# One matmul fewer in each half of the forward transform's 16-bin tile, two sums by VectorE instead

## The reference

```python
def fftconv(v, kf, skip):
    L = v.shape[1]
    vf = jnp.fft.rfft(v.astype(jnp.float32), n=2 * L, axis=1)
    y = jnp.fft.irfft(vf * kf[None], n=2 * L, axis=1)[:, :L]
    return y + v.astype(jnp.float32) * skip.astype(jnp.float32)

def hyena_mixer(u, x1, x2, kf, skip):
    z = fftconv(u, kf[:, 0], skip[0])
    z = x1.astype(jnp.float32) * z
    z = fftconv(z, kf[:, 1], skip[1])
    z = x2.astype(jnp.float32) * z
    return z.astype(u.dtype)
...
m = g_a * (y_a @ w_a) + g_b * (y_b @ w_b) + g_c * (y_c @ w_c)
return h + m @ w_out
```

## Time and profile before

| What | Value |
|---|---|
| Runs | 1127.41, 1128.18, 1128.9 us (median 1128.18) |
| Profiled execution, its own time | 1127.34 us |
| Its span | 1125.5 us |
| Granted TensorE clock, mean | 0.999 |
| TensorE busy | 1103.2 us, 98% of the span |
| VectorE busy | 772.3 us, 69% |
| ScalarE busy | 567.1 us, 50% |
| GpSimd busy | 61.9 us, 5% |
| HBM traffic | 178 GB/s over the span |

### The profile page before, as it was taken

One profiled execution on the slowest core, in us unless ns is written; L12 is line 12 of the kernel. 1 busy time (PEld: TensorE's weight loads), 2 busy tenths in 40 slices (PEclk: granted clock), 3 DMA queues, 4 the chain that ended last, 5 costly groups with the idle time before them and its releaser, 6 DMA issues.

```text
span 1125.5 us, 17228 instructions
## 1 busy us (share of the span) xinstructions
PE 1103.2 (98%) x7158; PEld 1005.7 (89%) x7158; DVE 772.3 (69%) x1151; ACT 567.1 (50%) x787; POOL 61.9 (5%) x98
## 2 busy tenths in 40 slices
PE   4999999999999999999999999999999999999997
PEld 2999999999999999999999988888888888888885
DVE  6778888778787688886888785554555455454654
ACT  6655555556545456555554564443444444444443
POOL 4030000300001200002000000000000000000000
PEclk9999999999999999999999999999999999999999
DMA  8744443644335534435543475555555555556652
GB/s 315 241 135 169 150 151 122 205 169 150 135 128 197 186 116 147 151 125 185 188 150 117 160 269 195 202 188 198 187 187 187 192 197 189 201 194 255 231 189 110
DMA packets 30494, 201.54 MB, mean 179 GB/s; under 512 B 3873, under 2 KB 4193, under 8 KB 7745
## 3 DMA queue, kind: packets, MB, share of 16 engines
q1 hardware_dynamic: 25024, 180.16, 45.4%
q0 software_dynamic: 5248, 19.77, 5.3%
q10 hardware_dynamic: 144, 0.52, 0.1%
HBM read 195.19 MB, written 5.24 MB: 178 GB/s over the span
## 4 chain that ended last, share of the span: by engine, by line
PE 98%; DVE 1%; ACT 0%; DMA 0%; issue 0%; DVEq 0%; ACTq 0%
PE ps L574 30%; PE ps L575 30%; PE ps L576 30%; PE ps L579 2%; PE ps L598 1%; PE ps L687 1%; PE ps L727 1%; PE ps L617 1%; PE ps L618 0%; PE ps L718 0%; PE ps L719 0%; PE ps L930 0%; PE ps L729 0%; DMA net<-net_in 0%; PE ps L735 0%; PE ps L737 0%
## 5 line engine op out<-in xcount | busy, mean ns | idle before, releaser
L1328 DVE TENSOR_TENSOR w_lo<-raw,w_hi 128x1024 fp32r<-128x1024 f32 x336 | 409.0, 1230 | 257.8 <-ACT w_hi L988 257.3
L988 ACT ACTIVATE w_hi<-raw 128x1024 fp32r<-128x1024 f32 x336 | 351.2, 1056 | 342.3 <-PE ps L576 340.1
L574 PE MATMUL ps<-xn_hi,w_hi 128*128 128x272 f32 (+2 forms) x1280 | 367.5, 287 | 0.0
L575 PE MATMUL ps<-xn_lo,w_hi 128*128 128x272 f32 (+2 forms) x1280 | 365.7, 286 | 0.0
L576 PE MATMUL ps<-xn_hi,w_lo 128*128 128x272 f32 (+2 forms) x1280 | 365.5, 286 | 0.0
L574 PEld LDWEIGHTS ps<-xn_hi,w_hi 128*128 128x128 f32 x1280 | 242.2, 189 | 2.0
L575 PEld LDWEIGHTS ps<-xn_lo,w_hi 128*128 128x128 f32 x1280 | 241.8, 189 | 0.7
L576 PEld LDWEIGHTS ps<-xn_hi,w_lo 128*128 128x128 f32 x1280 | 242.1, 189 | 0.0
L574 PE MATMUL ps<-w_hi,xg_hi 128*128 128x512 f32 x352 | 137.4, 390 | 0.0
L576 PE MATMUL ps<-w_hi,xg_lo 128*128 128x512 f32 x352 | 137.2, 390 | 0.0
L575 PE MATMUL ps<-w_lo,xg_hi 128*128 128x512 f32 x352 | 137.1, 390 | 0.0
(11 more groups left out here) (265 smaller groups left out, 1394.6 us busy)
## 6 DMA issues: line engine op xcount, KB each, us to landing
raw<-w_stream SPq DMA_DIRECT2D x168, 1024.0 KB, 4.9
branch_y<-ystage POOLq DMA_DIRECT2D x12, 256.0 KB, 3.9
y_raw<-branch_y POOLq DMA_DIRECT2D x3, 1024.0 KB, 7.0
xin<-x SPq DMA_DIRECT2D x2, 1024.0 KB, 6.4
w4s<-w POOLq DMA_DIRECT2D x16, 128.0 KB, 6.0
absd<-decay POOLq DMA_DIRECT2D x8, 256.0 KB, 6.2
h<-x POOLq DMA_DIRECT2D x2, 1024.0 KB, 8.2
rows_t<-rpb POOLq DMA_DIRECT2D x8, 219.0 KB, 6.2
```

Source lines behind the costliest of these rows:

```text
L574: mm(out_ap, a_hi, b_hi, start=first, stop=False)
L575: mm(out_ap, a_hi, b_lo, start=False, stop=False)
L988: A(w_hi[:, w % 2, part, :], raw[:, w % 4, 1024 * part:1024 * part + 1024], ACT.Copy).then_inc(hi_done, 1)
L1328: return V.tensor_tensor(dst, src, hi.bitcast(F32), ALU.subtract)
```

## The change

The 16-bin tile of the forward transforms gets a function of its own. The table `sym` gets 160 more columns: the 16 high columns and the 16 low columns for each of the two outputs, arranged so that for each output `ri` 48 columns starting at `7 * L + 16 * ri` hold the high part, another block, and the low part. A matmul of these 48 columns with `uT_hi` writes high by high into PSUM rows 0 to 15 and low by high into rows 32 to 47; rows 16 to 31 are not used. A second matmul adds high by `uT_lo` into rows 0 to 15, a third adds the stacked rest, whose table columns are padded with zeros to 48. ScalarE copies rows 32 to 47 of both outputs to a new tile `extra` (16 x 512); VectorE adds rows 0 to 15 to it, and the two multiplications read `extra` in place of PSUM. A new semaphore `fx_half` goes from the copy to the sum.

```diff
@@ constants()
-    sym = two_parts(np.concatenate([even[:128], odd[:128], back[0], back[1]], axis=1),
-                    np.concatenate([np.concatenate([even[128:], none]), np.concatenate([none, odd[128:]]), back[2]], axis=1))
+    hi, lo = two_parts(np.concatenate([even[:128], odd[:128], back[0], back[1]], axis=1),
+                       np.concatenate([np.concatenate([even[128:], none]), np.concatenate([none, odd[128:]]), back[2]], axis=1))
+    extra_bins = [part[:, at:at + NM] for part in (hi, lo) for at in (0, L)]
+    extra_rest = [np.pad(hi[:, at:at + NM], ((0, 0), (0, 2 * NM))) for at in (4 * L, 5 * L)]
+    sym = np.concatenate([hi] + extra_bins + extra_rest, axis=1), lo
@@ build()
-    sym_hi = place("sym_hi", [128, 7 * L], F32R)
+    sym_hi = place("sym_hi", [128, 7 * L + 10 * NM], F32R)
...
+    extra = place("extra", [128, 2, CC])
...
-            load_table("sym", sym_in, sym_hi[:, :], sym_lo[:, :], 7 * L)
+            load_table("sym", sym_in, sym_hi[:, :], sym_lo[:, :], 7 * L + 10 * NM)
@@ TensorE
+            def forward_extra():
+
+                for ri in range(2):
+                    out_ap, wide_ap = (ps[0:n, 4, CC * ri:CC * ri + CC] for n in (NM, 3 * NM))
+                    col, rest = 7 * L + NM * ri, 7 * L + 4 * NM + 3 * NM * ri
+                    mm(wide_ap, sym_hi[:, col:col + 3 * NM], uT_hi[:, ri, :], start=True, stop=False)
+                    mm(out_ap, sym_hi[:, col:col + NM], uT_lo[:, ri, :], start=False, stop=False)
+                    last = stacked(wide_ap, sym_hi[0:STACK, rest:rest + 3 * NM], uT_hi[0:STACK, 2, :], False, True)
+                last.then_inc(fwd_mm, 1)
...
                     if t == 5:
                         pe.wait_ge(y_full, c * 6 + 1)
-                        forward(2, 4)
+                        forward_extra()
...
                     if t == 13:
                         pe.wait_ge(y_full, c * 6 + 4)
-                        forward(2, 4)
+                        forward_extra()
@@ ScalarE, spectra()
                     n = TOK[f][1]
+                    if f == 2:
+                        act.wait_ge(fwd_mm, c * 6 + (3 * order + 3))
+                        A(extra[0:NM, :, :].rearrange("p r n -> p (r n)"), ps[2 * NM:3 * NM, 4, :], ACT.Copy).then_inc(fx_half, 1)
                     act.wait_ge(y_full, c * 6 + (3 * order + f + 1))
@@ VectorE, spectra()
                     bank = ps[0:n, 4 + f % 2, :].rearrange("p (r n) -> p r n", r=2)
+                    if f == 2:
+                        dve.wait_ge(fx_half, c * 2 + order + 1)
+                        link(V.tensor_tensor(extra[0:NM, :, :], extra[0:NM, :, :], bank, ALU.add))
+                        bank = extra[0:NM, :, :]
```

More of the change, by code:

```diff
@@ L388, in build @@
         fwd_mm = sem("fwd_mm")
+        fx_half = sem("fx_half")
         y_full = sem("y_full")
```

## The result

| | Kernel before | Changed kernel |
|---|---|---|
| Median of 13 runs | 1128.5 us (1127.41 to 1129.07) | 1130.69 us (1130.08 to 1131.52) |
| Ratio, 95% interval | | 1.0023 (1.0016 to 1.0031) |
| Profiled execution, its span | 1127.34, 1125.5 us | 1130.67, 1128.9 us |
| Mean granted clock | 0.999 | 0.998 |

The changed kernel is slower, by 2.6 us by the ratio (1.8 to 3.5). The forecast was 1130.9, within 1128.8 to 1132.6.

What follows compares the result with a forecast made beforehand. TensorE, busy 98% of the span, bounds the kernel, so its waits add in full: -0.23 + 3 x 0.52 + 3 x 0.33 + 0.44 = +2.76 us on 1128.18 gives 1130.9 us, range 1128.8 to 1132.6.

Steps and rivals of the forecast that it cites:

- What TensorE saves: 16-bin tile on TensorE: two matmuls fewer save 0.23 us per tile, 1.87 us over eight tiles.
- What ScalarE adds: Copy of 16 x 512 out of PSUM, 0.59 us, hidden in 5.67 us of ScalarE idle time; costed at nothing.
- The third rival: ScalarE's copy does not hide, or further waits arise: up to +6.9 us, 1135.1; chance 0.09.
- d: VectorE's delay from the added sum in each of the eight tiles: 0.71 us, bounds 0.60 and 0.75.
- The rival of d = 0.60: VectorE's sum is cheaper, the wait behind it being free: +2.0 us, 1130.2; chance 0.12.
- A: t = 8, `turn_p` of head 0 behind `normalized`, chunks 1 to 3: slack 0.19, late by 0.52 us each.
- B: t = 16, `fnet_channels` behind `fi_lo`, chunks 0 to 2: slack 0.38, late by 0.33 us each.
- C: t = 15, `attend(3)` in chunk 3: slack 0.27, late by 0.44 us; enough slack in chunk 0.
- The sum: Total over the kernel: -0.23 + 3 x 0.52 + 3 x 0.33 + 0.44 = +2.76 us.
- The factor of 7: Total over the seven late places written as 7d - 2.2, so VectorE's delay d counts seven times.
- the first term of -0.23: Chunk 0, order 0: the only tile whose TensorE saving, 0.23 us, is kept rather than lost at a wait.
- The first rival: VectorE's idle time ahead of the three places absorbs part of the delay: +0.1 us, 1128.3; chance 0.12.

Runs made afterwards that it cites:

- e1: Changed kernel without ScalarE's copy and VectorE's sum, multiplications reading PSUM; 1126.83 us against 1127.81 for the kernel before, ratio 0.9989.
- e10: Kernel before with only the longer table, its longer transfer and the shifted tiles; 1128.14 us against 1128.35, ratio 1.0001.
- e9: Changed kernel without ScalarE's copy, the sum taking the first product's tile instead; 1130.99 us, ratio 1.0027 to the kernel before.
- e12: Changed kernel with a second sum in chunk 3, order 1, alone; 1131.57 us, ratio 1.0033 to the kernel before.
- e2: Changed kernel with four matmuls kept, copy and sum made but unused, multiplications reading PSUM; 1130.92 us, ratio 1.0025 to the kernel before.
- e6: Changed kernel with the 16-bin tile's sum and multiplications moved earlier in both orders, low part left; 1126.59 us against 1128.22 for the kernel before.
- e3: Changed kernel with the sum done twice everywhere; 1136.6 us, ratio 1.0072 to the kernel before.
- e5: Changed kernel with the new form in order 1 alone, order 0 as before; 1129.63 us, ratio 1.0014 to the kernel before.
- e8: Changed kernel with only order 0's sum and multiplications moved earlier; 1128.68 us against 1128.35 for the kernel before, ratio 1.0005.
- e7: Kernel before with the 16-bin tile's multiplications moved earlier in both orders; 1128.07 us, ratio 0.9998.
- e11: Kernel before, unchanged, run and profiled a second time; 1127.91 us against 1128.35, ratio 0.9998.

## Why the prediction was right

- **What bounds the kernel:** right. e1 turned a shorter tile into a shorter total without any other change.
- **What TensorE saves:** slightly mis-sized. The prediction took 0.23 us for each tile, 1.87 in all; the eight tiles became 1.74 shorter (from 0.93 to 0.72 in order 0, from about 0.935 to 0.71 in order 1). It hardly mattered, because seven of the eight savings are lost at a wait anyway: the saving enters the sum once, as 0.21.
- **The longer table:** put at nothing, for a reason that concerns its loading alone. The kernels that have it lose some 0.3 us in small steps (e10). How much of that got past the waits of the changed kernel was not separated.
- **What ScalarE adds:** nothing, as costed (e9: 2.78 with no copy, 2.81 with it). The third rival falls with it.
- **What VectorE adds:** d = 0.71, as read. The Trainium skill's sentence in VectorE: DVE Perf Modes, The DRAIN you can't avoid, that a semaphore between chained operations is free, does not hold in this trace: two operations of 16 x 512 start 0.61 us apart without one and 0.71 with one. The rival of d = 0.60, +2.0 us, is 0.8 below the 2.81 found in the trace; the interval of the ratio alone could not exclude it.
- **Places and slacks:** the three places and the seven waits are right, and so is the single case of no wait, chunk 0 at t = 8. The sizes are less so. A was put at 0.52 and cost 0.45 to 0.47, B at 0.33 and cost 0.38 to 0.41, C at 0.44 and cost 0.45, each with the slower follow-up of the first matmul. At A the prediction allowed 0.16 us from VectorE's end to TensorE's work; the changed kernel shows 0.06 to the first transposition and 0.06 more for the pair, 0.12. At B it took the slack from the start of a matmul whose successor was only 0.06 behind it. The waits themselves were forecast at 0.75, 0.56 and 0.67 and took 0.65, 0.56 and 0.58.
- **The sum:** +2.76 forecast, +2.81 in the trace. That the two lie 0.05 apart is partly luck: over three chunks A was 0.19 too dear and B 0.20 too cheap. The factor of 7 is no luck: from d = 0.71 to 1.42 the loss grew by 4.97 (the fall of the clock aside), and one more sum in one place added 0.72 (e12). In e2, where the first term of -0.23 is missing, 3.0 was expected and 3.07 measured.
- **The first rival,** that idle time swallows a part: wrong, and for the reason given against it. The idle time of 1.34 us on VectorE is a wait for ScalarE's copy of VectorE's own result and moves along with it. e6 shows that it can be used, but only by putting other work into it.
- **From the profiled execution to the median:** the 0.84 us that the prediction added was needed. That execution was one whose clock rose early (last section).

## What to carry to other kernels

An engine that is busy for 69% of the span may have no slack at all where it matters: before giving it work, find each wait of the bounding engine behind the new instruction in its queue and take the slack, from the end of the operation that ends the wait to the start of the work that needs it, less what a restart costs (0.06 to 0.10 us here); time saved ahead of such a wait is not saved. An idle time inside a chain that feeds itself does not absorb a delay, it moves with it; but independent work of the same queue (half a slab split here) can be put into it, and then the same change that cost 2.6 us gains 1.7.

## What the runs showed of the hardware

**A clock that fell behind a wait of one microsecond.** TensorE in e3, chunk 3: the wait ahead of `attend(3)`, the matmuls behind it, and where they become fast again.

```profile
642.39 0.45 PE L750 MATMUL ps<-pT_hi,v_two 128*128 128x256 f32 x1 [1.06 <-DVE o L1651]
642.64 0.42 PE L751 MATMUL ps<-pT_lo,v_two 128*128 128x256 f32 x1
642.86 0.42 PE L752 MATMUL ps<-pT_rest,vT_rest 80*64 80x256 f32 x1
...
646.03 0.28 PE L579 MATMUL ps<-xn_hi,w_hi 128*128 128x256 f32 x1
646.15 0.28 PE L580 MATMUL ps<-xn_lo,w_hi 128*128 128x256 f32 x1
```

Busy times by stretch in e3; the number before the last two is the granted clock:

```profile
585.50:590.00 4.50, 4.50 (x39) 4.42 (x38) 4.49 (x6) 3.27 (x8) 0.00 (x0) 1.00 0.53 217
642.30:646.00 3.70, 3.61 (x17) 3.61 (x18) 3.67 (x9) 0.85 (x2) 0.00 (x0) 0.54 0.03 11
646.00:650.00 4.00, 4.00 (x36) 4.00 (x35) 3.44 (x6) 1.06 (x1) 0.55 (x1) 1.00 0.07 27
```

For 3.6 us matmuls of 256 columns started 0.215 us apart in place of 0.12, at a granted clock of 0.54, the level of 1.2 GHz: seventeen of them at 0.095 more are the 1.6 us. It is no matter of the wait's length alone. In the same execution the wait of 1.15 us ahead of `turn_p` at 585.03 left the clock at 1.00 (first row). Nor is it one of place and length together, since e12 waits as long at the same place with no fall, as its timeline of TensorE shows:

```profile
637.66 0.38 PE L750 MATMUL ps<-pT_hi,v_two 128*128 128x256 f32 x1 [1.07 <-DVE o L1652]
637.88 0.28 PE L751 MATMUL ps<-pT_lo,v_two 128*128 128x256 f32 x1
638.00 0.28 PE L752 MATMUL ps<-pT_rest,vT_rest 80*64 80x256 f32 x1
```

e3 has ten waits in its chunks, the three at `turn_p` about 1.1 us each; e12 has seven, six of them of at most 0.4. Whether that or chance decides stays open. The executions without a trace speak for chance: two of e12's six have a mean granted clock of 0.997 and took 1.5 and 2.0 us more than the profiled one, and of e3's five two have 0.996 and 0.997, three 0.998 or 0.999. No execution of another kernel has less than 0.998. In numbers, a wait printed as 1.06 us was followed by 1.6 us of loss from the clock.

**The clock rises at another moment from one execution to the next.** The first slab starts between 24.1 and 24.9 us, at the lower level. TensorE in the profile of the kernel before, and in that of the changed kernel:

```profile
26.86 0.38 PE L574 MATMUL ps<-xn_hi,w_hi 128*128 128x272 f32 x1
27.07 0.28 PE L575 MATMUL ps<-xn_lo,w_hi 128*128 128x272 f32 x1
27.20 0.29 PE L576 MATMUL ps<-xn_hi,w_lo 128*128 128x272 f32 x1
```

```profile
27.74 0.41 PE L579 MATMUL ps<-xn_hi,w_hi 128*128 128x272 f32 x1
27.97 0.31 PE L580 MATMUL ps<-xn_lo,w_hi 128*128 128x272 f32 x1
28.11 0.29 PE L581 MATMUL ps<-xn_hi,w_lo 128*128 128x272 f32 x1
```

Matmuls are 0.227 apart until the rise and 0.126 after it. (The profile's granted clock is printed as 1.00 ahead of the rise too, so here the level is told by the distance alone.) It came at 27.0 in the one and at 28.0 in the other, at 29.6 in e5 and at 30.4 in e8. Each matmul more at the lower level costs 0.10 us, and eleven more make 1.1. That is most of what moves the first line of the table from -0.11 (e7) to 1.16 (e5), in a part of the program that none of these kernels changes; e11, the kernel before once more, has 0.58 there. With e8 (1.63) the spread is 1.7 us, over half of what this change costs. A difference of two profiled spans of this kernel is therefore worth little below that, while the distance between two landmarks behind the first slab repeats within 0.01 us over 560 us in e7 and e11.

The Trainium skill (TensorE: Matmul & The Clock Gate, Part 1) says that the number of slow matmuls at the start varies between runs of one kernel. The traces agree: the kernel before had its rise at 27.0 in one profile and at about 28.1 in the other (e11).
